# Four plain pairs instead of six in three feed-forward stages, and another order of the seven products

## The reference, cut to what matters

```python
D_MODEL, SEQ, DEPTH, D_FF = 1024, 512, 2, 2816

def swiglu(h, w_in, w_out):
    gu = h @ w_in
    a, b = gu[..., :D_FF], gu[..., D_FF:]
    return (jax.nn.silu(a) * b) @ w_out

for l in range(DEPTH):
    x = x + 0.5 * swiglu(rmsnorm(x, norm_ffn1[l]), w_ffn1_in[l], w_ffn1_out[l])
    h = rmsnorm(x, norm_mix[l])
    x = x + mixing_sublayer(h, w_in[l], ...)
    x = x + 0.5 * swiglu(rmsnorm(x, norm_ffn2[l]), w_ffn2_in[l], w_ffn2_out[l])
```

## Time and profile before

| | us |
|---|---|
| median of 3 runs | 2751.94 (2750.74 to 2753.53) |
| the profiled execution | 2751.83 |
| its span (first to last instruction) | 2750.0 |
| PE busy in the span | 2737.1 |
| DVE busy | 1808.9 |
| ACT busy | 1199.0 |
| granted PE clock | 1.00 throughout |

### The profile page before, as it was taken

One profiled execution on the slowest core, in us unless ns is written; L12 is line 12 of the kernel. 1 busy time (PEld: TensorE's weight loads), 2 busy tenths in 40 slices (PEclk: granted clock), 3 DMA queues, 4 the chain that ended last, 5 costly groups with the idle time before them and its releaser, 6 DMA issues.

```text
span 2750.0 us, 40964 instructions
## 1 busy us (share of the span) xinstructions
PE 2737.1 (100%) x15496; PEld 2374.2 (86%) x15496; DVE 1808.9 (66%) x2665; ACT 1199.0 (44%) x1874; POOL 114.8 (4%) x132
## 2 busy tenths in 40 slices
PE   9999999999999999999999999999999999999998
PEld 7999888878889988899888888889998887888787
DVE  7887455675678845788454567567783665676565
ACT  5444323364344433344333346334443344754474
POOL 0110000000001100011000000001110000000000
PEclk9999999999999999999999999999999999999999
DMA  5685232213347832488323222326763331133112
GB/s 183 179 211 140 90 123 85 73 58 93 99 138 203 203 111 91 131 208 201 115 94 111 80 66 70 99 89 173 200 180 110 92 92 47 47 100 93 61 49 82
DMA packets 96157, 320.90 MB, mean 117 GB/s; under 512 B 9760, under 2 KB 9888, under 8 KB 95776
## 3 DMA queue, kind: packets, MB, share of 16 engines
q1 hardware_dynamic: 67824, 245.41, 29.1%
q0 software_dynamic: 26624, 67.12, 10.9%
q10 hardware_dynamic: 1584, 6.64, 0.7%
HBM read 317.03 MB, written 2.10 MB: 116 GB/s over the span
## 4 chain that ended last, share of the span: by engine, by line
PE 94%; DVE 3%; DMA 1%; ACT 1%; issue 1%; ACTq 0%; SPq 0%; DVEq 0%
PE bank L693 19%; PE bank L695 19%; PE bank L694 19%; PE bank L772 8%; PE bank L774 8%; PE bank L773 8%; PE bank L852 1%; PE bank L853 1%; PE bank L854 1%; PE bank L1136 1%; PE bank L937 1%; PE bank L1358 1%; PE bank L1037 1%; PE bank L1147 1%; PE bank L1360 1%
## 5 line engine op out<-in xcount | busy, mean ns | idle before, releaser
L693 PE MATMUL bank<-xh,wh 128*128 128x512 f32 x1536 | 605.5, 394 | 0.3 <-DVE wl L2121 0.3
L695 PE MATMUL bank<-xh,wl 128*128 128x512 f32 x1536 | 598.9, 390 | 0.0
L694 PE MATMUL bank<-xl,wh 128*128 128x512 f32 x1536 | 598.2, 389 | 0.0
L2121 DVE TENSOR_TENSOR wl<-raw,wh 128x1024 fp32r<-128x1024 f32 x332 | 404.0, 1220 | 243.0 <-ACT wh L1475 242.3
L1475 ACT ACTIVATE wh<-raw 128x1024 fp32r<-128x1024 f32 x332 | 349.2, 1054 | 390.2 <-PE bank L695 189.0
L772 PE MATMUL bank<-urh,wh 128*128 128x256 f32 x1280 | 362.7, 283 | 0.0
L774 PE MATMUL bank<-urh,wl 128*128 128x256 f32 x1280 | 362.4, 283 | 0.0
L773 PE MATMUL bank<-url,wh 128*128 128x256 f32 x1280 | 362.4, 283 | 0.0
L693 PEld LDWEIGHTS bank<-xh,wh 128*128 128x128 f32 x1536 | 288.7, 188 | 61.9 <-issue 3.8
L695 PEld LDWEIGHTS bank<-xh,wl 128*128 128x128 f32 x1536 | 288.4, 188 | 60.9
L694 PEld LDWEIGHTS bank<-xl,wh 128*128 128x128 f32 x1536 | 288.8, 188 | 57.5
(11 more groups left out here) (476 smaller groups left out, 4690.7 us busy)
## 6 DMA issues: line engine op xcount, KB each, us to landing
raw<-stream SPq DMA_DIRECT2D x460, 512.0 KB, 3.6
s<-stream POOLq DMA_DIRECT2D x128, 512.0 KB, 5.7
dec<-decay ACTq DMA_DIRECT2D x2, 1024.0 KB, 6.4
out<-x SPq DMA_DIRECT2D x3, 512.0 KB, 2.6
x<-x_t ACTq DMA_DIRECT2D x2, 512.0 KB, 6.2
x<-x_t SPq DMA_DIRECT2D x2, 512.0 KB, 8.3
rp<-rope ACTq DMA_DIRECT2D x2, 512.0 KB, 7.4
g_post<-rows ACTq DMA_DIRECT2D x2, 512.0 KB, 3.6
```

The costliest lines, as they stand in the source:

```text
L693: pe.matmul(o, wh[:, s, c], rhs_h, start=first, stop=False)
L694: pe.matmul(o, wh[:, s, c], rhs_l, start=False, stop=False)
L695: return pe.matmul(o, wl[:, s, c], rhs_h, start=False, stop=last)
L2121: dve.tensor_tensor(wl[:, at.slot, :], raw[:, at.raw, :], wh[:, at.slot, :].bitcast(F32), ALU.subtract).then_inc(split_lo, 1)
```

## The change

Three edits:

- `PLAINS` goes from (6, 6, 6, 6) to (6, 4, 4, 4), and `SEVENS` from (16, 16, 16, 16) to (16, 18, 18, 18): in blocks 1, 2 and 3 two more tiles are made with seven products. With four plain pairs DVE and ACT take another written-out order ahead of the seven-product pairs (the branch `if PLAINS[f] == 4`, which was there already and is among the functions printed above); block 0 keeps that of six.
- The order inside a seven-product pair becomes Q1, Q4, Q7, Q5, Q2, Q6, Q3: the two products of `s31` come ahead of the second panel and of `s24`. ACT and DVE split `s31` ahead of `s24` accordingly, and DVE's sums A to D move.
- The plain load of `s31` is begun by ACT (`load_s31`), for pairs 0 and 1 right after ACT's B11, and from then on in step c for pair c + 2. GpSimd keeps the adding transfer alone, and the loads have a semaphore for each of the two buffers.

```diff
 BLOCK = PANEL // 2
-PLAINS = (6, 6, 6, 6)
+PLAINS = (6, 4, 4, 4)
 SEVENS = tuple(KF - n for n in PLAINS)
...
         nx_act = Steps(sem("normed_act"), "H11", "H21", "H22", "HT1", "HT2", "HT3", "HT4")
-        seven_pe = Steps(sem("seven_products_pe"), "Q1", "Q6", "Q3", "Q5")
-        sum_load, sum_add = sem("weights_loaded"), [sem(f"weights_added_{q}") for q in range(2)]
-        w_hi = Steps(sem("weight_sums_act"), "S24", "S31")
-        w_lo = Steps(sem("weight_rests_dve"), "S24", "S31")
+        seven_pe = Steps(sem("seven_products_pe"), "Q1", "Q5", "Q6", "Q3")
+        sum_load, sum_add = ([sem(f"weights_{what}_{q}") for q in range(2)] for what in ("loaded", "added"))
+        w_hi = Steps(sem("weight_sums_act"), "S31", "S24")
+        w_lo = Steps(sem("weight_rests_dve"), "S31", "S24")
         parts = Steps(sem("first_product_act"), "Q1")
...

-            def load(f, c):
-                at = starts[f] + 2 * (PLAINS[f] + c)
-                if c >= 2:
-                    gp.wait_ge(*w_lo.at(SEVEN_AT[f] + c - 2, "S31"))
-                elif c == 0:
-                    gp.wait_ge(*nx.at(f, "N7"))
-                    gp.wait_ge(*nx_act.at(f, "H11"))
-                gp.dma_start(s31[:, c % 2, :, :], stream[at.done(0)].rearrange("p (a b) -> p a b", b=BLOCK))\
-                  .then_inc(sum_load, 16)
-
             def add(f, c):
                 at = starts[f] + 2 * (PLAINS[f] + c) + 1
-                gp.wait_ge(sum_load, (SEVEN_AT[f] + c + 1) * 16)
+                gp.wait_ge(sum_load[c % 2], (SEVEN_AT[f] // 2 + c // 2 + 1) * 16)
                 gp.dma_start(s31[:, c % 2, :, :], twice(stream[at.done(0)][:, 0:BLOCK]), accum_op=ALU.add)\
...
             for f in range(2 * DEPTH):
-                load(f, 0)
                 for c in range(SEVENS[f]):
                     add(f, c)
-                    if c < SEVENS[f] - 1:
-                        load(f, c + 1)

...
                     product(q, "Q4", c, "A22", "T4").then_inc(panel_done, 1)
+                    pe.wait_ge(*w_lo.at(r(), "S31"))
+                    product(q, "Q7", c, "S3", "T3")
+                    product(q, "Q5", c, "S1", "T1").then_inc(seven_pe.sem, 1)
                     panel_ready(at + 1)
...
                     product(q, "Q3", c, "S4", "B22").then_inc(seven_pe.sem, 1)
-                    pe.wait_ge(*w_lo.at(r(), "S31"))
-                    product(q, "Q7", c, "S3", "T3")
-                    product(q, "Q5", c, "S1", "T1").then_inc(seven_pe.sem, 1)

...

+                def load_s31(i, c):
+                    if i is not None or c >= 2:
+                        act.wait_ge(*w_lo.at(r(i, c - 2), "S31"))
+                    act.dma_start(s31[:, c % 2, :, :],
+                                  stream[panel_at(base, i, c).done(0)].rearrange("p (a b) -> p a b", b=BLOCK))\
+                       .then_inc(sum_load[c % 2], 16)
+
                 def step(i, c):
-                    high_s31(i, c)
-                    first_copy(i, c)
+                    high_s24(i, c)
+                    if i is not None or c < SEVENS[f] - 2:
+                        load_s31(i, c + 2)
                     if i is not None or c > 0:
                         gate(i, c - 1)
+                    first_copy(i, c)
                     if i is not None or c < SEVENS[f] - 1:
...
                         high_a12(i, c + 1)
-                        high_s24(i, c + 1)
+                        high_s31(i, c + 1)

...
                     moving_high("B11", XN[0, 0], "N7")
+                    load_s31(None, 0)
+                    load_s31(None, 1)
                     high(idx + 7)
...
                     high_a12(None, 0)
-                    high_s24(None, 0)
+                    high_s31(None, 0)
                     silu(3)
...
                     moving_high("B11", XN[0, 0], "N7")
+                    load_s31(None, 0)
+                    load_s31(None, 1)
                     high(idx + 7)
...
                     high_a12(None, 0)
-                    high_s24(None, 0)
+                    high_s31(None, 0)
                     silu(5)
...
                 elif kt < U_FIRST + U_RING:
-                    act.wait_ge(*seven_pe.at(SEVEN_AT[f] + SEVENS[f] - 1, "Q5"))
+                    act.wait_ge(*seven_pe.at(SEVEN_AT[f] + SEVENS[f] - 1, "Q3"))
                 else:
...
                     dve.wait_ge(*added.at(r(i, c), "B"))
+                    dve.wait_ge(*seven_pe.at(r(i, c), "Q3"))
                     dve.tensor_tensor(gate_w2[:, q, 1, :], psum[:, place("Q3", q)], w34[:, 1, :], ALU.add)                       .then_inc(added.sem, 1)
...
                 def outputs(i, c):
-                    add_b(i, c)
                     add_c(i, c)
...

-                def step(i, c):
+                def step(i, c, last=None):
                     if i is not None or c > 0:
-                        add_b(i, c - 1)
                         add_c(i, c - 1)
-                    low_s31(i, c)
+                        add_d(i, c - 1)
+                    low_s24(i, c)
                     if i is not None or c > 0:
-                        add_d(i, c - 1)
                         hidden_tile(i, c - 1)
...
                         sum_4(i, c + 1)
+                        low_s31(i, c + 1)
+                    if last:
+                        last()
                     add_a(i, c)
-                    if i is not None or c < SEVENS[f] - 1:
-                        low_s24(i, c + 1)
+                    add_b(i, c)

...
                     evicted(3)
-                    low_s24(None, 0)
+                    low_s31(None, 0)
                     product(3)
...
                     evicted(5)
-                    low_s24(None, 0)
+                    low_s31(None, 0)
                     product(5)
...
                 step(None, end - 1)
-                step(None, end)
-                low(out0)
-                hidden_low(f, 0)
-                hidden_low(f, 1)
+                step(None, end, lambda: (low(out0), hidden_low(f, 0), hidden_low(f, 1)))
                 outputs(None, end)
```

## The result

| | before | after |
|---|---|---|
| median, us (runs) | 2751.53 (2750.41 to 2753.53, 7) | 2761.76 (2754.58 to 2764.15, 7) |
| the profiled execution, its span | 2750.0 | 2760.9 |
| ratio after / before | | 1.0034, 95% interval 1.0025 to 1.0044 |

The forecast was 2748.6, the range ended at 2752.8. The time lies 9 us above the range.

The account below looks back on a forecast made before the run. PE was taken as the bound, busy 2737.1 of 2750.0 us. 2751.83 - 4.80 (plain pairs) - 0.64 (waits) + 2.13 (starts) = 2748.5 for the profiled execution, 2748.6 us as median; range 2746.2 to 2752.8.

Parts of the forecast that it names:

- The pace of PE: In blocks 1, 2, 3, six pairs go from 10.88 to 10.08 us on PE: 4.80 us less.
- The rival that columns alone set the pace: Seven-product pairs: 256 columns take half of 0.2267 us, a pair 9.52, six save 8.2; 2745.2 us, chance 0.01.
- The starts: Blocks 1 to 3, first Q7: PE waits 0.71 us for DVE's low part of `s31`; 2.1 us come back.
- The order of the products, ACT's issues: Seven-product pairs: the new order leaves PE's work equal; ACT's issue, 0.5 us a pair, is hidden by its idle time.
- The load of `s31`: Begun by ACT two pairs ahead, ready with 2 us left at the worst landing times, 6 at the median, every pair.
- P: Start of pair c on PE; ACT's load issue was put at about P + 1.2, pair c + 2 at P + 20.16.
- the lead: DVE begins each block some way ahead and loses 0.8 us a pair; in blocks 1 and 2 this lasts.
- The waits of blocks 0 and 3 should go: 0.64 us less: PE's waits in the sixteen seven-product pairs, 0.27 us in block 0 and 0.37 in block 3, should vanish.
- DVE's low part of `s31` ready some 5 us ahead of its need: Sign expected in the loop of seven-product pairs if the forecast held.
- Rows 4: Profile rows of block 0's `s31` transfers, read as 21.73 us for two pairs, 10.87 a pair against PE's 10.08.
- the transfers keep the pace: Rival: PE waits in every seven-product pair once load and adding transfer take over 18.9 us; 2804 us, chance 0.07.
- a fifth of the pairs, 11 us: 2759.6: Milder case of the transfers rival: a fifth of the 70 seven-product pairs take 10.87 us; rival's chance 0.07.

## Why the prediction was wrong, point by point

- **The pace of PE**: right. Plain pairs 10.88 and seven-product pairs 10.08 where nothing waits; -4.80 is there in the windows, though the times of the run with the plain pairs alone show at most 3.6 of it. The rival that columns alone set the pace is out: 18 pairs in 181.43. The prediction's figure from the Trainium skill, "TensorE: Matmul & The Clock Gate" (Back-to-back issue gap), is no guide here either. That section gives the formula for an isolated matmul and says that it has no budget for weight loads, of which this kernel has one for each matmul.
- **The starts**: right in place, size and releaser. In block 1 PE's 24th and 25th matmul of the first seven-product pair stand 0.79 us apart in the rows below, where 0.12 is the pace: 0.67 lost there and 0.75 in the whole pair, for a forecast of 0.71. None in block 0.
- **The order of the products, ACT's issues**: right. GpSimd's loads with the new order lose nothing but the starts; ACT's issue takes 0.34 us.
- **The load of `s31`**: here it fell. The sentence is "2 us are left at the worst row and 6 at the median, in every pair alike, since the load hangs on PE's own pace". Two things are wrong in it.
  - First the durations. 4.7 and 7.9 us were read where the load starts 5.1 us behind the other buffer's adding transfer. Where it starts 2.6 behind, they take 7.1 and 9.1: the medians of now are about the worst rows of then. Starting the load 3.3 us earlier after the sum gave the two transfers 3.9 us more. The issue came at P + 2.1 in the median and not at P + 1.2. So the sum of `s24` begins at about P + 2.1 + 7.8 + 9.4 = P + 19.3, where the forecast had P + 13.8, and PE waits from P + 19.4 on (20.16 - 0.75). Even by the prediction's own worst rows, 1.6 us were left ahead of Q1 (20.16 - 18.6) and not 2.
  - Second what the load hangs on. ACT also waits for DVE's reading of `s31`, at least 3.0 us behind the start of a sum that itself waits for the transfer. So the sum of the terms had to be made round the circle, 3.0 + 0.2 + load + adding transfer against 20.16, and not from P. The point from which it decides is then 17.0 us for the two transfers, not 18.9. The prediction's worst rows (7.4 + 9.4 = 16.8) stood at that edge already, before GpSimd's and DVE's answers. And behind it a pair's loss is not paid once: it adds up, pair after pair, until the lead is gone.
- **"The waits of blocks 0 and 3 should go: 0.64 us less"**: they became 3.13 and 4.76, and block 2 got 3.89. The sign "DVE's low part of `s31` ready some 5 us ahead of its need" failed with them: it is ready 3.03 us or more behind a sum that leads PE's pair by 0.75 to 4.4 us, for a need at 2.88.
- **Rows 4** were read as the pace of the loop, 10.87 us a pair. They show one bad stretch. In the four blocks of before the mean circle is 20.53, 20.21, 20.08 and 20.55 us: the transfers keep a pace within 0.2 us a pair of PE's everywhere, in blocks 1 and 2 too, where I took the lead for lasting. That should have been the warning.
- **The chances**: the rival "the transfers keep the pace" named the mechanism, and its milder case ("a fifth of the pairs, 11 us: 2759.6") is what came, with PE's waits nearly all at Q1. It had 0.07. That the margin rested on landing times measured under another spacing of the transfers was a reason for some 0.3 and a range up to its price.

PE's timeline in after, block 1, ahead of the first Q7:

```profile
793.57 0.28 PE L761 MATMUL bank<-xh,wl 128*128 128x256 f32 x1
...
794.36 0.39 PE L759 MATMUL bank<-xh,wh 128*128 128x256 f32 x1 [0.51 <-DVE wl L2251]
```

## What stays open

Why ACT's loads make the circle half a microsecond longer than GpSimd's, though GpSimd's start even closer behind the adding transfer, is located (0.29 in the reading, behind late panels; 0.19 in the transfers, 0.04 at the issue; one execution each) but not explained: why the panels and the adding transfer land later beside ACT's load no run separates. The run with the load ahead of `s24` excludes only its place in ACT's row. Also open is why the kernels without waits gain less in their times than in their windows. The Trainium skill, "DMA: Bandwidth & Descriptors" (Issuing engine by pattern), calls transfers started by the sync and scalar engines generally faster. The landings of the load and the adding transfer with GpSimd's loads (us, min/median/max) are

```profile
DMA to landing us min/median/max: 3.6/8.0/9.0
```

```profile
DMA to landing us min/median/max: 5.5/8.4/9.5
```

against 7.1 and 9.1 in after: ACT's load is faster by 0.9 us, the adding transfer behind it slower by 0.7, and the kernel 0.4% slower.

## What to carry to other kernels

Where a buffer's refill waits for its last reader, and that reader's chain starts with the refill's landing, add up the whole circle and compare it with the time that the loop has for it; slack against the matrix engine alone missed it here. A landing time is worth only what the spacing of the transfers is worth under which it was read: begun 3.3 us earlier, into a time when others ran, the two transfers here took 3.9 us more. If the circle is too long, a further buffer opens it. The other queue (GpSimd's) shortened it here, from 20.92 to 20.40 us, to what the lead could cover, and did not open it; an issue 0.2 us earlier did not help.

## What the runs showed of the hardware

- Two 512 KB transfers for one buffer, beside two panel loads of 512 KB, all within 10.08 us: 13.4 us from issue to use when the load starts 5.1 us behind the other buffer's adding transfer, 17.1 to 17.3 when it starts 1.7 to 2.6 us behind. A load of 256 KB, started 4.7 us behind, landed in 4.5 us; one of 512 KB, started 5.1 behind, in 4.7; one of 512 KB, started 2.6 behind, in 7.1 (medians).
- An addition on GpSimd (128x1024, two operands in SBUF) takes 2.4 to 3.7 us and can hold up a two-operand subtraction on DVE until it ends: 3.46 us instead of 1.21 where the subtraction began 0.50 us behind the addition.
